# Sample attention of a hybrid trunk: the compression's first layer in fp32, two buffers for the selected branch's rows, and one constant carried over from the prompt's compression

## The reference, cut to what matters

```python
def compress_kv(kv, pe, w1, b1, w2, b2):
    ...                                       # ch: 256 chunks of 16 rows, keys and values, 2 heads of 64
    w1r = w1.reshape(2, 2, CMP_STRIDE, HEAD_DIM, CMP_HIDDEN)
    h_a = jnp.einsum('...nsckd,csdh->...nckh', ch, w1r[:, 0])
    h_b = jnp.einsum('...nsckd,csdh->...nckh', ch, w1r[:, 1])
    c0 = jnp.einsum('crd,crdh->ch', pe, w1.reshape(2, CMP_BLOCK, HEAD_DIM, CMP_HIDDEN)) + b1
    hid = jax.nn.gelu(h_a[..., :-1, :, :, :] + h_b[..., 1:, :, :, :] + c0[:, None, :])
    return jnp.einsum('...nckh,chd->...nckd', hid, w2) + b2[:, None, :]
```

## Time and profile before

| | |
|---|---|
| runs of the kernel before | 2741.89 us median of 3 (2740.26 to 2746.6) |
| the profiled execution | 2743.73 us, of which 2741.5 us is the span from first to last instruction |
| PE, busy over the span | 2254.1 us (82%) |
| DVE / ACT / POOL, busy | 1361.8 us (50%) / 997.5 us (36%) / 217.1 us (8%) |
| DMA | 462.59 MB, 169 GB/s over the span |
| mean granted PE clock | 0.894 of full speed |
| sample stage | about 981 us to 1540 us of the span |

### The profile page before, as it was taken

One profiled execution on the slowest core, in us unless ns is written; L12 is line 12 of the kernel. 1 busy time (PEld: TensorE's weight loads), 2 busy tenths in 40 slices (PEclk: granted clock), 3 DMA queues, 4 the chain that ended last, 5 costly groups with the idle time before them and its releaser, 6 DMA issues.

```text
span 2741.5 us, 34279 instructions
## 1 busy us (share of the span) xinstructions
PE 2254.1 (82%) x12983; PEld 1749.2 (64%) x12983; DVE 1361.8 (50%) x2157; ACT 997.5 (36%) x1278; POOL 217.1 (8%) x191
## 2 busy tenths in 40 slices
PE   7999999968898968888878245989934999999980
PEld 7999999964434446666656134654513888888870
DVE  4310333114565524444444494332334999999975
ACT  3111111112232314333333443112414787777762
POOL 0000000000221200000000001000012111111102
PEclk9999999967998979999899577899966999999995
DMA  4232333323000041333332305342207999999957
GB/s 155 97 132 69 123 135 127 122 70 124 12 5 5 8 170 62 147 155 154 146 160 95 128 17 164 94 152 77 99 33 308 415 413 413 416 412 415 412 216 291
DMA packets 109049, 462.59 MB, mean 169 GB/s; under 512 B 21072, under 2 KB 53760, under 8 KB 91064
## 3 DMA queue, kind: packets, MB, share of 16 engines
q1 hardware_dynamic: 73400, 321.70, 30.8%
q0 software_dynamic: 12448, 93.35, 8.3%
q10 hardware_dynamic: 23104, 46.20, 4.5%
HBM read 389.05 MB, written 79.05 MB: 171 GB/s over the span
## 4 chain that ended last, share of the span: by engine, by line
PE 67%; DVE 12%; DMA 9%; issue 5%; ACT 3%; POOL 1%; SPq 1%; ACTq 0%; DVEq 0%; POOLq 0%; PEldq 0%
PE ps L252 11%; PE ps L254 11%; PE ps L253 11%; PE ps L2416 5%; PE ps L2341 4%; PE ps L1457 4%; DMA arena<-in_cache_slc,arena 3%; PE ps L1105 2%; PE ps L1087 2%; DVE c_x_low L1668 1%; DMA arena<-in_rope 1%; PE ps L2835 1%; PE ps L1442 1%; DMA arena<-scratch_zT 1%; PE ps L1583 1%
## 5 line engine op out<-in xcount | busy, mean ns | idle before, releaser
L2967 DVE TENSOR_TENSOR e_low<-e_raw,e_high 128x2048 fp32r<-128x2048 f32 x192 | 430.5, 2283 | 55.7 <-ACT e_high L2905 55.7
L2905 ACT ACTIVATE e_high<-e_raw 128x2048 fp32r<-128x2048 f32 x192 | 356.8, 1912 | 18.9 <-ACT arena L2924 18.9
L252 PE MATMUL ps<-e_high,e_x_high 128*128 128x512 f32 x512 | 203.1, 397 | 10.1 <-DVE e_low L2967 7.5
L254 PE MATMUL ps<-e_high,e_x_low 128*128 128x512 f32 x512 | 200.7, 392 | 0.0
L253 PE MATMUL ps<-e_low,e_x_high 128*128 128x512 f32 x512 | 200.5, 392 | 0.0
L252 PE MATMUL ps<-h_high,wc_high 128*128 128x352 f32 x576 | 187.1, 325 | 1.3 <-ACTq L610 1.3
L253 PE MATMUL ps<-h_low,wc_high 128*128 128x352 f32 x576 | 185.6, 322 | 0.0
L254 PE MATMUL ps<-h_high,wc_low 128*128 128x352 f32 x576 | 185.4, 322 | 0.0
L252 PE MATMUL ps<-w_high,h_high 128*128 128x256 f32 (+1 forms) x576 | 174.1, 302 | 7.8 <-DVE w_low L436 4.9
L254 PE MATMUL ps<-w_high,h_low 128*128 128x256 f32 (+1 forms) x576 | 172.9, 300 | 0.0
L253 PE MATMUL ps<-w_low,h_high 128*128 128x256 f32 (+1 forms) x576 | 172.8, 300 | 0.0
(11 more groups left out here) (536 smaller groups left out, 4535.1 us busy)
## 6 DMA issues: line engine op xcount, KB each, us to landing
e_raw<-in_w_gate SPq DMA_DIRECT2D x32, 2048.0 KB, 10.2
e_raw<-in_w_up SPq DMA_DIRECT2D x32, 2048.0 KB, 9.7
e_raw<-in_w_down SPq DMA_DIRECT2D x32, 2048.0 KB, 10.6
scratch_yb<-arena ACTq DMA_DIRECT2D x32, 512.0 KB, 10.9
scratch_zT<-arena ACTq DMA_DIRECT2D x24, 528.0 KB, 2.7
wc_raw<-in_w_cols SPq DMA_DIRECT2D x24, 512.0 KB, 5.7
arena<-in_x_all SPq DMA_DIRECT2D x18, 512.0 KB, 3.5
scratch_yb<-arena SPq DMA_DIRECT2D x16, 512.0 KB, 5.4
```

Of the source, the lines that this page charges most:

```text
L252: nc.tensor.matmul(out, ah, bh, start=start, stop=False)
L254: return nc.tensor.matmul(out, al, bh, start=False, stop=stop)
L2905: nc.scalar.activation(high[m][:, c], raw[m][u][:, c], ACT.Copy).then_inc(high_ready[m], 1)
L2967: nc.vector.tensor_tensor(low[m][u][:, c], raw[m][u][:, c], high[m][:, c].bitcast(F32), ALU.subtract).then_inc(split_ready[m], 1)
```

## The change

It does four things. `c0` moves to a `k.keep` buffer, which the prompt's compression writes and the sample stage reads, so the sample stage neither loads `b1` and `pe` nor computes `c0`. The first layer is one fp32 matmul for each weight tile in place of three F32R ones, so `w1` isn't split, the transposed rows are copied once, by ACT (`copies`), and `lows` is gone. The bank is free, and a piece ready, when ACT's copy is done (`copied`). `xs` becomes two sets, used in turn, and POOL's gathers are put in another order. The first transposition no longer waits for the weights; the first `hidden` does.

```diff
-def prompt_compress_stage(k, d, res, ident):
+def prompt_compress_stage(k, d, res, ident, c0):
...
-    comp = Compress(k, d, "pcmp", 1, n, ident, res["ckT"], res["cv"])
+    comp = Compress(k, d, "pcmp", 1, n, ident, res["ckT"], res["cv"], c0)
...
-def sample_stage(k, d, stash, ident):
+def sample_stage(k, d, stash, ident, c0):
...
-    xc, xs, xw = k.buf(2, CHW), k.buf(2, CHW), k.buf(4, KVW)
+    xc, xs_pair, xw = k.buf(2, CHW), k.buf(2, 2, CHW), k.buf(4, KVW)
...
         gather(0, xc, xc_loaded, "cache_cmp")
-        gather(0, xs, xs_loaded, "cache_slc")
+        gather(0, xs_pair[:, 0], xs_loaded[0], "cache_slc")
         for b in range(1, NSEQ):
+            if b >= 2:
+                pool.wait_ge(pv_summed, b - 1)
+            gather(b, xs_pair[:, b % 2], xs_loaded[b % 2], "cache_slc")
             pool.wait_ge(turned, 16 * b)
             gather(b, xc, xc_loaded, "cache_cmp")
-            pool.wait_ge(pv_summed, b)
-            gather(b, xs, xs_loaded, "cache_slc")
...
     def tensor(pe):
-        pe.wait_ge(params_loaded, 96)
-        for c in range(2):
-            for j in range(16):
-                ins = nc.tensor.matmul(ps[:, 7, c:c + 1], w1_raw[:, c, j], pe_in[:, c, j:j + 1],
-                                       start=(j == 0), stop=(j == 15))
-        ins.then_inc(c0_summed, 1)
-
         def turn(b, c, pieces):
...
                 if n >= 4:
-                    pe.wait_ge(low_copied, n - 3)
+                    pe.wait_ge(copied, n - 3)
...
-                ins = None
-                for a, v in ((w1_high, x_high), (w1_high, x_low), (w1_low, x_high)):
-                    ins = nc.tensor.matmul(ps[:, 4 + c, 0:n], a[:, c, m], v[:, c, s2, KVH * part:KVH * part + n],
-                                           start=(m == 0 and a is w1_high and v is x_high),
-                                           stop=(m == 15 and a is w1_low))
+                ins = nc.tensor.matmul(ps[:, 4 + c, 0:n], w1[:, c, m], turned_x[:, c, s2, KVH * part:KVH * part + n],
+                                       start=(m == 0), stop=(m == 15))
...
-        pe.wait_ge(w1_split, 1)
         turn(0, 0, range(8))
+        pe.wait_ge(params_loaded, 64)
         hidden(0, 0, 0)
...
     def scalar(act):
...
-                nc.scalar.activation(x_high[:, c, s2], ps[:, s2 % 4], ACT.Copy).then_inc(high_copied, 1)
+                nc.scalar.activation(turned_x[:, c, s2], ps[:, s2 % 4], ACT.Copy).then_inc(copied, 1)
...
-        def lows(b, c, pieces):
-            for s2 in pieces:
-                dve.wait_ge(high_copied, 16 * b + 8 * c + s2 + 1)
-                nc.vector.tensor_tensor(x_low[:, c, s2], ps[:, s2 % 4], x_high[:, c, s2].bitcast(F32), ALU.subtract
-                                        ).then_inc(low_copied, 1)
...
-            if more:
-                lows(b + 1, 0, range(2))
...
-            if more:
-                lows(b + 1, 0, range(2, 8))
...
-            if more:
-                lows(b + 1, 1, range(8))
...
+        c0 = k.keep(2)
         top = k.high
```

More of the change, by code:

```diff
@@ L104, in __init__ @@
                     self.projected[name] = places.enter_context(nc.sbuf_tensor(name, [P, words], dtype))
[L105 to L111, removed]
         slots = [(m, u) for m in range(3) for u in range(2)]
@@ L1315, in sample_stage @@
     SELW, ALLW = 2 * 512 + NNEW, 2 * 512 + P + 2 * NNEW
[L1316 to L1321, removed]
-    xc, xs, xw = k.buf(2, CHW), k.buf(2, CHW), k.buf(4, KVW)
-    w2, b1, pe_in = k.buf(2, HD), k.buf(2), k.buf(2, 16)
-    b2k, b2v, c0 = k.buf(1), k.buf(P), k.buf(2)
+    turned_x = k.buf(2, 8, KVH * CN)
+    kT = turned_x[:, 0].rearrange("p s n -> p (s n)")
+    w1 = k.buf(2, 16, P)
+    xc, xs_pair, xw = k.buf(2, CHW), k.buf(2, 2, CHW), k.buf(4, KVW)
+    w2, b2k, b2v = k.buf(2, HD), k.buf(1), k.buf(P)
     x, t, hid = (k.buf(KVH * CN) for _ in range(3))
@@ L1342, in sample_stage @@
     chunk_ready = sem("chunk_ready")
-    xc_loaded, xs_loaded = k.own_sem("s_xc_loaded"), k.own_sem("s_xs_loaded")
+    xc_loaded, xs_loaded = k.own_sem("s_xc_loaded"), [k.own_sem(f"s_xs_loaded{u}") for u in range(2)]
     small_loaded, dve_step = sem("small_loaded"), sem("step")
     stored = [sem(f"stored{u}") for u in (0, 1)]
-    c0_summed, c0_ready, w1_ready, w1_split = sem("c0_summed"), sem("c0_ready"), sem("w1_high"), sem("w1_split")
-    turned, high_copied, low_copied = sem("chunks_turned"), sem("chunks_high"), sem("chunks_low")
+    turned, copied = sem("chunks_turned"), sem("chunks_copied")
     hid_summed, cubed, sig_ready, hid_ready = sem("hid_summed"), sem("cubed"), sem("sigmoid"), sem("hid_ready")
@@ L1362, in sync @@
     def sync(sp):
-        for to, src in ((w1_raw, d["cmp_w1"].rearrange("p (c j n) -> p c j n", c=2, j=16)),
-                        (w2, d["cmp_w2"].rearrange("p (c n) -> p c n", c=2)), (b1, d["cmp_b1"]),
-                        (pe_in, d["pe"].rearrange("p (c j) -> p c j", c=2)), (b2k, d["cmp_b2k"]),
+        for to, src in ((w1, d["cmp_w1"].rearrange("p (c j n) -> p c j n", c=2, j=16)),
+                        (w2, d["cmp_w2"].rearrange("p (c n) -> p c n", c=2)), (b2k, d["cmp_b2k"]),
                         (b2v, d["cmp_b2v"].partition_broadcast(P).rearrange("p o n -> p (o n)"))):
@@ L1592, in scalar, with copies @@
     def scalar(act):
-        act.wait_ge(params_loaded, 96)
-        for c in range(2):
-            nc.scalar.activation(w1_high[:, c].rearrange("p j n -> p (j n)"),
-                                 w1_raw[:, c].rearrange("p j n -> p (j n)"), ACT.Copy).then_inc(w1_ready, 1)
-        def highs(b, c, pieces):
+        def copies(b, c, pieces):
             if b:
@@ L1608, in sigmoid @@
                                  ).then_inc(sig_ready, 1)
-        highs(0, 0, range(8))
-        highs(0, 1, range(8))
+        copies(0, 0, range(8))
+        copies(0, 1, range(8))
         sigmoid(0, 0)
@@ L1631, in scalar @@
             if more:
-                highs(b + 1, 0, range(8))
-                highs(b + 1, 1, range(8))
+                copies(b + 1, 0, range(8))
+                copies(b + 1, 1, range(8))
             act.wait_ge(nb_ready, b + 1)
@@ L1708, in final @@
             ins.then_inc(out_ready, 1)
-        lows(0, 0, range(8))
-        lows(0, 1, range(8))
         cube(0, 0)
```

28 lines of the change are left out of this document (11 added, 17 removed).

## The result

The changed kernel takes 2716.3 us, the median of 8 runs (2712.1 to 2719.9), beside 2740.2 for the kernel before (8 runs): a ratio of 0.9913, 95% interval 0.9896 to 0.9929, or 19 to 29 us less. I had forecast 8 us less.

A forecast was written before the change was run, and what follows sets the result against it. PE was taken to set each round, with gaps. 43.6 us lost to fp32, less gains of 4.9, 1.4, 14.8, 3.5, 13.3, 9.8 and 4.0, gave -8.1: from 2741.89 to 2733.8 us, range 2723 to 2748.

The forecast's parts named there:

- half clock at the keys: PE's key transposes after the wait for selected rows: half clock goes in four rounds, 0.9 us each, 3.5 us gained.
- The clock: 4 us gained, 0 to 8: First layer: shorter idle time ahead removes half-clock stretches; half of five times 1.6 us credited.
- All clock falls close: Rival: the whole 8 us of first-layer clock and 1.5 at the keys in four rounds return, 2727.4 us; chance 0.16.
- The first layer in fp32: First layer on PE: one fp32 matmul per tile replaces three F32R ones, a loss of 43.6 us, up to 47.
- four whole passes: Rival: in the first layer fp32 costs four F32R pitches a tile, 59.0 us more, giving 2749.2 us; chance 0.08.
- The start: Start of the sample stage: first transposition waits only for the gather of `xc`, at 1005.7; 4.9 us gained.
- Two sets of selected rows: PE before its keys: 14.8 us of waiting for `xs` and about 3.5 us of half clock go.
- the second set's own worth: Waits before the keys: what exceeds the 2.7 us the longer first layer hides, about 1 us in two rounds.
- The eviction: Copies of turned rows without DVE's subtraction: 13.3 us gained at the keys and 9.8 at the values.
- ACT and PE alternate: Rival: eviction copies take 0.60 us, not 0.515, with no clock credit, giving 2745.5 us; chance 0.24.
- `xc` becomes the wait: Rival: the gather of compressed rows is late, costing 3 us and 2 us of clock credit, 2739 us; chance 0.07.
- The round: Sign in the trace: a sample-stage round of about 64 us instead of 65 confirms the sum.

The follow-up runs named there:

- e7: Changed kernel with three F32R products of one rounded copy per weight tile and one set of selected rows, ACT's eviction kept: 2701.0 us, 0.9840 of the kernel before.
- e3: Changed kernel with three F32R products of one rounded copy per weight tile instead of fp32, compressed rows gathered first: 2683.1 us, 0.9798 of the kernel before.
- e5: Changed kernel with one set of selected rows and DVE's second pass releasing each bank, fp32 kept: 2752.7 us, 1.0041 of the kernel before.
- e2: Changed kernel with DVE passing over each bank again behind ACT's copy, only this pass releasing the bank: 2744.0 us, 1.0017 of the kernel before.
- e1: Changed kernel with a single set of selected rows and the gathers in their old order: 2720.9 us, 0.9938 of the kernel before.
- e4: Changed kernel with the next keys' first layer, second part, cut 3, 1, 3, 1 tiles, five moved to later places: 2675.6 us, 0.9764 of the kernel before.
- e10: Changed kernel with two of eight first-layer tiles moved from before the mask's spread to before the probabilities' transposes: 2689.6 us, 0.9798 of the kernel before.
- e11: Changed kernel with one first-layer tile moved from before the mask's spread to behind the probabilities' transposes: 2697.9 us, 0.9818 of the kernel before.

## Why the prediction was wrong

The sum's terms beside the pair of profiled runs. The loop's part is the differences of the windows, summed over the rounds; what is at half clock is a window's length less its length in a round at full clock.

| term | forecast | measured |
|---|---|---|
| first layer in fp32, at full clock | +43.6 | +41.4 |
| start and first sequence's values | -6.3 | -8.3 |
| waits for the selected rows | -14.8 | -15.3 |
| half clock at the keys | -3.5 | -3.3 |
| keys' eviction | -13.3 | -15.3 |
| values' eviction | -9.8 | -10.2 |
| half clock in the first layer | -4.0 | -13.3 |
| half clock elsewhere (mask, turn, PV) | 0 | -2.4 |
| sum | -8.1 | -26.7 |

The sample stage as a whole is 27.3 us shorter in that pair, the spans differ by 30.1, the medians by 23.9. The two clock rows for the first layer and elsewhere hold 11.7 of the 18.6 us by which the sum missed; the other six are off by 2.2 at most.

**The step that failed** is "The clock: 4 us gained, 0 to 8". It was mis-sized in two ways. First, I counted five stretches of the first layer at half clock, "in four rounds and once in the first sequence". There were eight. The three that I missed are tails: they begin in PV and run on into the next sequence's second half, as in the window 1097.05:1110.97 above, where I had looked only behind the turn. The full price of eight, 13.3 us, lies 5 beyond my upper bound. Second, I credited half of the five, with the shorter idle time ahead of the first layer as the reason, and all five closed. For the four behind the turn that reason is possible but not the only one: they are absent with ACT's eviction alone (e7, e3) and with fp32 alone (e5, e2), and the changed kernel has both. The three tails need fp32 and two sets together, an effect that no term of mine has. So a part of the credit belongs to the term that I had only as a loss: from e3 to the changed kernel fp32 costs 41 us of matmul and gets some 8 to 10 of them back by the clock. I also wrote of the fall before PV that what it stands behind doesn't change; the windows of PV and the turned probabilities are 1.8 us shorter in all seven rounds together, so that was nearly right. The rival "All clock falls close" (2727.4) had the mechanism, with the same five stretches, and is still 11 us above the result.

**The first layer in fp32.** Right in kind, 2 us too dear. Sixteen records of 512 columns take 7.13 us, of 510 columns 7.11: less the first distance, their pitch is 0.429 and 0.428, or 0.858 and 0.855 a matmul. The merge stage's mean of 0.432 that I used contains a stretch of 7.11 us, which has such a longer first distance. The misfit of F32R at 510 columns is not there. The Trainium skill's page "FP8 and Floating Point Precision", section "TensorE Precision Notes", gives true fp32 four passes; an estimate of four F32R pitches a tile puts the loss at 59 us by it. The trace does not agree: it has 3.78 and 3.65 times an F32R pitch, and 41 us. The rival "four whole passes" falls.

**The start.** Right: the first transposition waits for `xc` alone. It starts at 1003.06, where I said 1005.7; 1.4 us of this the stages ahead of it were earlier. The gather landed 11.9 us after its issue, before 13.1.

**Two sets of selected rows.** The waits went as forecast, and with them the half clock behind them. That "the second set's own worth" is about 1 us in two rounds was too low: 4.7 by the medians, 10.3 by the seven rounds. In e1 each of the three rounds of the window with a wait, of 0.7 to 1.3 us, ends in a half clock that lasts through PV into the next first layer; that the wait brings this about is likely, but no run shows it apart.

**The eviction.** Right: the first layer 5.53 us behind its first transposition, where I said 5.7, before 7.70; the exponentials 2.5 us behind the mask's last transpose (2.6). "ACT and PE alternate" falls: four copies take 2.06 us as before. "`xc` becomes the wait" falls too: PE's transposes wait for that gather at the start only.

**The round** of "about 64 us" was the sign that I named, and 61.4 shows the sum wrong at once.

What stays open: why the half clock of PV runs on into the next first layer in some rounds and ends with PV in others, in one kernel whose rounds differ by 0.6 us at most (e1), and whether it is the fp32 products themselves or the length of the round that takes the tails away. No run here tells these apart, and each pattern is read from one execution.

## What to carry to other kernels

Before crediting or charging a clock, cut a whole round into windows at the same places in every round and write down each window's length against its shortest one: that finds all the stretches at half clock, the tails that begin in another step among them, and it is the upper bound of the credit. An edit that makes PE's work longer can pay for a part of itself where the clock is at half, so its price is measured with the clock, not by the pitch alone. And once the queues' waits are gone, work that nobody waits for belongs into PE's idle time: a few tiles moved were worth more here (41 us, e4) than the whole change (24).

## What the runs showed of the hardware

- Records of fp32 matmuls start 0.428 us apart at 510 columns and 0.429 at 512, after a first distance of 0.53; F32R ones of 510 were 3% dearer than of 512.
- PE's clock stood at half at PV in rounds whose longest idle time of PE was 2.01 us; 1.74 us of matmuls moved into that gap took the half clock from PV in every round (e10).
- A part of the time comes in the form of a pattern over rounds: every second round in e3 and e11, each round alike in the changed kernel. One round's windows are therefore not enough to price a term.
